# A hybrid decoder step on one core: gated outputs' parts in their own tiles, a rebuilt program end, page numbers read before the wait for old pages, key and value turns in two pairs of banks

## What is computed

```
h = RMSNorm(x);  p = h @ w_in                     # one projection for both groups
attention group (8 heads x 128): prompt: causal softmax; samples: 256 past positions from
    paged caches cache_k, cache_v (2 pages of 128 per sequence, by page_table) and the own 8
Gated DeltaNet group (8 heads x 128): causal conv + SiLU, chunked delta rule,
    gated RMSNorm with SiLU(z)
x = x + concat(attention, gated) @ w_out
x = x + ConvFFN(RMSNorm(x))                       # up, causal conv of width 3, SiLU(gate)*value, down
y = RMSNorm(x)                                    # final norm, over the 2048 channels of a token
```

## Time and profile before

| what | value |
|---|---|
| median of three runs | 1676.88 us (1676.06 to 1678.0) |
| profiled execution | 1671.89 us |
| its span, first to last instruction | 1670.2 us |
| TensorE busy | 1634.9 us (98%) |
| VectorE, ScalarE, GpSimd busy | 1048.6, 616.9, 237.4 us |
| granted TensorE clock, mean | 0.997 |
| DMA | 255.12 MB, mean 153 GB/s |

### The profile page before, as it was taken

One profiled execution on the slowest core, in us unless ns is written; L12 is line 12 of the kernel. 1 busy time (PEld: TensorE's weight loads), 2 busy tenths in 40 slices (PEclk: granted clock), 3 DMA queues, 4 the chain that ended last, 5 costly groups with the idle time before them and its releaser, 6 DMA issues.

```text
span 1670.2 us, 30879 instructions
## 1 busy us (share of the span) xinstructions
PE 1634.9 (98%) x12884; PEld 1581.8 (95%) x12884; DVE 1048.6 (63%) x1702; ACT 616.9 (37%) x783; POOL 237.4 (14%) x371
## 2 busy tenths in 40 slices
PE   8999999999999999999999999999999999999996
PEld 7999889988998888999999999999999999999996
DVE  5676688656544454676666666666666666666665
ACT  6444323432343343553333333333333333333334
POOL 1122342122211012210101010101010101010004
PEclk9999999999999999999999999999999999999998
DMA  8434355435846556454444444444444444445442
GB/s 251 126 115 116 107 152 153 116 108 171 274 137 204 176 182 190 153 157 147 151 150 152 151 152 149 148 148 151 151 151 152 147 149 148 150 149 154 141 150 83
DMA packets 230171, 255.12 MB, mean 153 GB/s; under 512 B 9036, under 2 KB 220558, under 8 KB 229712
## 3 DMA queue, kind: packets, MB, share of 16 engines
q1 hardware_dynamic: 217488, 220.16, 43.0%
q0 software_dynamic: 9856, 31.71, 6.2%
q10 hardware_dynamic: 2688, 1.27, 0.3%
HBM read 242.00 MB, written 11.12 MB: 152 GB/s over the span
## 4 chain that ended last, share of the span: by engine, by line
PE 90%; DVE 2%; issue 2%; DMA 2%; POOL 2%; ACT 0%; POOLq 0%; SPq 0%; DVEq 0%; ACTq 0%
PE ps_proj L1698 22%; PE ps_proj L1699 21%; PE ps_proj L1700 21%; PE ps_small L1699 6%; PE ps_small L1698 6%; PE ps_small L1700 6%; PE ps_small L1735 2%; DMA k_pages<-in_cache_k_dram 1%; PE ps_small L1874 0%; PE ps_small L1964 0%; PE ps_small L1864 0%; DVE state_s L1123 0%; DVE w_lo L1128 0%; DMA x_raw<-in_x_sample_dram 0%; DMA state_s<-in_state_gdn_dram 0%
## 5 line engine op out<-in xcount | busy, mean ns | idle before, releaser
L1698 PE MATMUL ps_proj<-x_hi,w_hi 128*128 128x320 f32 x2560 | 808.9, 316 | 3.4 <-issue 3.4
L1700 PE MATMUL ps_proj<-x_hi,w_lo 128*128 128x320 f32 x2560 | 791.3, 309 | 0.0
L1699 PE MATMUL ps_proj<-x_lo,w_hi 128*128 128x320 f32 x2560 | 791.2, 309 | 0.0
L791 ACT ACTIVATE w_hi<-w_raw 128x1024 fp32r<-128x1024 f32 x408 | 432.0, 1059 | 748.5 <-PE ps_proj L1700 550.6
L1128 DVE TENSOR_TENSOR w_lo<-w_raw,w_hi 128x1024 fp32r<-128x1024 f32 x408 | 498.4, 1224 | 310.5 <-ACT w_hi L791 310.1
L1698 PEld LDWEIGHTS ps_proj<-x_hi,w_hi 128*128 128x128 f32 x2560 | 481.0, 188 | 18.8 <-issue 15.6
L1699 PEld LDWEIGHTS ps_proj<-x_lo,w_hi 128*128 128x128 f32 x2560 | 481.3, 188 | 1.5 <-issue 1.4
L1700 PEld LDWEIGHTS ps_proj<-x_hi,w_lo 128*128 128x128 f32 x2560 | 480.8, 188 | 0.0
L1698 PE MATMUL ps_small<-hid_hi,w_hi 128*128 128x320 f32 x704 | 217.9, 309 | 0.0
L1700 PE MATMUL ps_small<-hid_hi,w_lo 128*128 128x320 f32 x704 | 217.6, 309 | 0.0
L1699 PE MATMUL ps_small<-hid_lo,w_hi 128*128 128x320 f32 x704 | 217.5, 309 | 0.0
(11 more groups left out here) (329 smaller groups left out, 1070.3 us busy)
## 6 DMA issues: line engine op xcount, KB each, us to landing
w_raw<-in_w_up_dram SPq DMA_DIRECT2D x176, 512.0 KB, 3.6
w_raw<-in_w_in_dram SPq DMA_DIRECT2D x112, 512.0 KB, 3.8
w_raw<-in_w_down_dram SPq DMA_DIRECT2D x88, 512.0 KB, 3.6
w_raw<-in_w_out_dram SPq DMA_DIRECT2D x32, 512.0 KB, 4.3
k_pages<-in_cache_k_dram POOLq DMA_DIRECT2D x32, 256.0 KB, 3.7
v_pages<-in_cache_v_dram POOLq DMA_DIRECT2D x32, 256.0 KB, 4.3
state_s<-in_state_gdn_dram POOLq DMA_DIRECT2D x10, 512.0 KB, 5.8
out_ss_dram<-state_s POOLq DMA_DIRECT2D x8, 512.0 KB, 4.4
```

Source lines behind the costliest of these rows:

```text
L791: act.activation(whi[:, slot], raw[:, slot], ACT.Copy).then_inc(hi_done, 1)
L1698: pe.matmul(o, hi, rhs_hi[:, k0 + kk_, :], start=first and kk_ == 0, stop=False)
L1699: pe.matmul(o, hi, rhs_lo[:, k0 + kk_, :], start=False, stop=False)
L1700: ins = pe.matmul(o, lo, rhs_hi[:, k0 + kk_, :], start=False, stop=last and kk_ == CQ - 1)
```

## The change

Four edits:

1. `mg` writes to tiles of its own. `gated_hi` lies over the keys and values of group 0's region, whose last reader is the score step of sequence 7, and `gated_lo` over `z_gate` itself. The steps stand five and three chunks before wg, and wait for that score step in place of the chunk. `fload` writes to the same place as `gated_lo`, so it moves from wg + 1 to wa0 + 1 and waits until the wg chunks are done.
2. The keys and values of units 0 and 2 are turned into banks b2 and b3, those of unit 1 into b0 and b1. The first scores wait for the copy of unit 1, and the first turn of the score weights (`T`, which writes b2) for the copy of unit 2.
3. The two page numbers are read before the wait for the old pages, and the two loads issued one behind the other.
4. The program end. `turn_y(2)` stands before the last down chunk. The last chunk signals after its first tile of 128 channels, and its two tiles are added, weighed and squared one by one. The sums over partitions are formed as columns, 128 tokens x 1, by twelve small products with the squares as the stationary operand, so no transposes follow. The root is a `Sqrt` on ScalarE, with a first `Sqrt` on constants during the last down chunks, and a reciprocal on VectorE. The rows are scaled in pieces, the last quarter straight from PSUM, and go out in six transfers in place of three.

```diff
-    slots[FIRST["wg"] - 1, PARTS - 1] += [("A", "mg", 0), ("V", "mg", 0), ("A", "mg", 1), ("V", "mg", 1)]
-    slots[FIRST["wg"] + 1, 0].append(("A", "fload"))
+    for g in range(2):
+        slots[FIRST["wg"] - 5 + 2 * g, PARTS - 1] += [("A", "mg", g), ("V", "mg", g)]
+    slots[FIRST["wa0"] + 1, 0].append(("A", "fload"))
...
+    zhi = nc.alloc_sbuf_tensor_at("gated_hi", [P, 8, TOK], F32R, offset=mixer_at + 4 * 4 * TOK)
+    zlo = nc.alloc_sbuf_tensor_at("gated_lo", [P, 8, TOK], F32R, offset=zz_at)
...
+            for ready, count, out, tile_ in (
+                    ("y0", 1, O["yp"][0, 0:P, 0:1024], yo[:, 0, 0:1024]),
+                    ("y1", 1, O["yp"][0, P:SEQ, 0:1024], yo[:, 1, 0:1024]),
+                    ("y0", 2, O["yp"][0, 0:P, 1024:2048], yo[:, 0, 1024:2048]),
+                    ("y1", 2, O["yp"][0, P:SEQ, 1024:2048], yo[:, 1, 1024:2048]),
+                    ("y0", 3, samples[:, 0:1024], yo[0:NS, 2, 0:1024]),
+                    ("y0", 4, samples[:, 1024:2048], yo[NS:P, 2, 0:1024])):
                 sp.wait_ge(fin[ready], count)
...
-                    act.activation(kst[0:n, (3 * g + t) % 2].rearrange("p h d -> p (h d)"), b0[0:n], ACT.Copy)
-                    finish(act.activation(vt[0:n, t].rearrange("p h d -> p (h d)"), b1[0:n], ACT.Copy))
+                    k_bank, v_bank = (b0, b1) if t == 1 else (b2, b3)
...
                     after(act, "V", "oz", g, 2)
-                    act.wait_ge(mm_done, FIRST["wg"])
-                    finish(act.activation(xhi[:, 8 + 4 * g:12 + 4 * g, :], zz[:, 4 * g:4 * g + 4, :], ACT.Copy))
+                    after(act, "P", "SS", 0, DB - 1)
+                    finish(act.activation(zhi[:, 4 * g:4 * g + 4, :], zz[:, 4 * g:4 * g + 4, :], ACT.Copy))
...
+            def last_tile_square(j):
+                act.wait_ge(fin["x7"], j + 1)
+                act.wait_ge(fin["sqs"], 6)
+                act.activation(sqb[:, 1, j, :], xres[:, 14 + j, :], ACT.Square).then_inc(fin["sq"], 1)
...
+            act.wait_ge(fin["ms"], 1)
+            act.activation(sm("ssx"), sm("ssx"), ACT.Sqrt).then_inc(fin["mr"], 1)
             act.wait_ge(fin["r"], 1)
-            act.wait_ge(fin["ev"], 12)
-            act.activation(yo[:, 1, :], yo[:, 1, :], ACT.Copy, scale=sm("rsx", P, 1, 2)).then_inc(fin["y1"], 1)
+            act.wait_ge(fin["ev"], 9)
+            root_ = sm("rsx", P, 1, 2)
+            act.activation(yo[:, 1, 0:1024], yo[:, 1, 0:1024], ACT.Copy, scale=root_).then_inc(fin["y1"], 1)
+            act.activation(yo[:, 1, 1024:1536], yo[:, 1, 1024:1536], ACT.Copy, scale=root_)
+            act.wait_ge(fin["t"], 11)
+            act.activation(yo[:, 1, 1536:2048], psA[:, 1, :], ACT.Copy, scale=root_).then_inc(fin["y1"], 1)
...
-                    after(pe, *(("A", "kv", g, t - 1) if t else ("V", "hb", g)))
-                    for kind, bank in ((1, b0), (2, b1)):
+                    after(pe, *(("A", "kv", g, 0) if t == 2 else ("V", "hb", g)))
+                    for kind, bank in ((1, b0 if t == 1 else b2), (2, b1 if t == 1 else b3)):
...
-                        after(pe, "A", "kv", g, 2)
+                        after(pe, "A", "kv", g, 1)
...
+                def add(x, first, last):
+                    for t, rows in ((0, slice(0, P)), (1, slice(0, P)), (2, slice(0, NS)), (2, slice(NS, P))):
+                        n, c0 = unit(t)
+                        ins = pe.matmul(token_sum(t)[rows, :], x[:, c0:c0 + n], sm("tmp", P, 0, 1), start=first, stop=last)
+                    return ins
...
+                    page = [pool.value_load(ptab[0:1, 2 * b + i:2 * b + i + 1], min_val=0, max_val=n_pool - 1) for i in range(2)]
                     if name == "pk":
...
                     for i in range(2):
-                        page = pool.value_load(ptab[0:1, 2 * b + i:2 * b + i + 1], min_val=0, max_val=n_pool - 1)
-                        src = cache[0].rearrange("n s h d -> n s (h d)")[bass.DynSlice(page, 1), :, 512 * g:512 * g + 512]
+                        src = cache[0].rearrange("n s h d -> n s (h d)")[bass.DynSlice(page[i], 1), :, 512 * g:512 * g + 512]
...
-            pool.wait_ge(fin["mr"], 1)
-            power(sm("rsx", P, 0, 2), sm("ssx", P, 0, 2), P, 2)
-            power(sm("rsx", NS, 2, 3), sm("ssx", NS, 2, 3), NS, 1).then_inc(fin["r"], 1)
```

More of the change, by code:

```diff
@@ L1098, in _ @@
                     new_rows_out(4)
+                    act.activation(sm("so", P, 0, 4), C("ones", P, 4), ACT.Sqrt)
                 elif d < 7:
@@ L1688, in finish, with products @@
                 ins.then_inc(done["P"], 1)
-            def products(c, slot, out_bank, k0, first, last, rhs_hi, rhs_lo, between=lambda r: None):
+            def products(c, slot, out_bank, k0, first, last, rhs_hi, rhs_lo, between=lambda r: None, first_tile=None):
                 pe.wait_ge(lo_done, c + 1)
@@ L1703, in products @@
                             between(done_ * PARTS // (2 * CQ) - 1)
+                    if j == 0 and first_tile is not None:
+                        ins.then_inc(first_tile, 1)
                 ins.then_inc(mm_done, 1)
@@ L2014, in step @@
                     after(pe, "V", "N", g, h)
+                    if h == 0:
+                        after(pe, "A", "kv", g, 2)
                     s_ = sc[:, h % 2]
@@ L2160, in turn_y @@
                     for j in range(4):
-                        ins = turn(psA[0:n, t, j * P:(j + 1) * P], xn[:, q % 2, j, c0:c0 + n], P)
+                        out, tile_ = psA[y_rows(t, q), t, j * P:(j + 1) * P], xn[:, q % 2, j, c0:c0 + n]
+                        if y_rows(t, q).start:
+                            ins = pe.matmul(out, tile_, C("ident"), start=True, stop=True)
+                        else:
+                            ins = turn(out, tile_, P)
                     ins.then_inc(fin["t"], 1)
             for d in range(8):
-                down(c + d, NB - 1, d, (NB - 1) % 2)
+                down(c + d, NB - 1, d, (NB - 1) % 2, fin["half"] if d == 7 else None)
                 if d == 0:
@@ L2173, in _ @@
                     turn_y(d // 2 - 1)
-            turn_y(2)
-            pe.wait_ge(fin["ne"], 5)
-            last_sum()
+                elif d == 6:
+                    turn_y(2)
+            last_sums()
             turn_y(3)
-            pe.wait_ge(fin["ms"], 1)
-            pe.wait_ge(f["add"], NB * 8 + 2)
-            for t in range(3):
-                n, c0 = unit(t)
-                ins = pe.transpose(b0[0:n, t:t + 1], rs2[0:1, c0:c0 + n], C("ident", 1, 1))
-            ins.then_inc(fin["mt"], 1)
         @block.gpsimd
```

120 lines of the change are left out of this document (80 added, 40 removed).

## The result

The changed kernel takes 1659.53 us (median of 4 runs, 1658.61 to 1660.96), the kernel before beside it 1676.47 (4 runs, 1675.29 to 1678.0). The ratio is 0.9897, 95% interval 0.9885 to 0.991. It is 16.9 us faster. The profiled execution has a span of 1659.3 us, 10.9 less than before. So profile and profile differ by about what was forecast, and the medians by more. The experiments are about that difference.

A forecast was written before the change was run, and what follows sets the result against it. TensorE was busy 1634.9 of 1670.2 us, so only its idle time and the program end could pay. Terms 3.2 + 3.0 + 0 + 2.3 + 0.2 + 2.8 = 11.5, taken as 11.4: median 1665.5 us, range 1662.5 to 1670.5.

The forecast's parts named there:

- Turns of keys and values: First scores of group 1: TensorE's wait for unit 2's copy goes whole, 3.2 us won, bounds 3.2 and 2.3.
- rival 1: Waits come back elsewhere (fload issues, score scale without cover, pages bound by bandwidth): 6.5 us won, 1670.4; chance 0.17.
- Gated parts: Start of wg: TensorE's 2.99 us idle, caused by VectorE's subtractions, goes; 3.0 us won, bounds 3.0 and 0.
- rival 4: At wg the 2.99 us idle are issue and stay: 8.4 us won, 1668.5; chance 0.04.
- Moved loads: fload's ten issues on ScalarE, ahead of the key copy: value 0, 0.7 us of cover; bounds 0 and 2 us lost.
- Page numbers: TensorE's four waits for key pages shrink through earlier reads and loads: 2.3 us won, bounds 3.3 and 1.0.
- Program end: Behind TensorE's last product: scaling and first transfer start sooner, 0.2 us added for shorter rows; 2.8 us won, bounds 4.0 and 1.0.
- rivals 2 and 3: Rival 2: program end gives nothing, 1668.2 us, chance 0.07. Rival 3: output pieces do not overlap, 1687.5 us, chance 0.02.
- I subtract the same microseconds from both: Whole kernel: the same savings, 11.4 us, taken from the profiled execution (1671.89 us) and from the runs' median (1676.88).
- value pages: TensorE's wait for value pages, 0.2 us, likely gone too, since the first is issued 0.9 us sooner.

The follow-up runs named there:

- the three sets: Runs of the unchanged kernel before, timed beside three groups of four follow-up kernels each: medians 1675.84, 1676.31 and 1675.68 us.
- Gated parts and banks: Kernel before with only the first and second edits, key pages and program end as before: 1665.63 us, ratio 0.9941.
- the parts alone: Kernel before with one edit each: gated parts 1673.05 us, key and value banks 1671.22, page numbers 1673.44, program end 1672.86.

## Why the prediction was right or wrong

**Right: the waits and the end.** Turns of keys and values: 3.2 forecast, the wait is gone; rival 1's lack of cover for the score scale did not come. Gated parts: 3.0 forecast, 3.0 gone (the other 0.4 us of that row stays, ahead of wa1), and the cause was VectorE, so rival 4 falls. Moved loads: 0 forecast, 0.7 us of cover forecast and 0.7 found. Page numbers: 2.3 forecast, 3.3 less 1.0 is 2.3. That it fits so well is luck: these waits sum to 2.2 to 3.3 us in the profiles with the old order and to anything from 0 to 2.1 in those with the new one. Program end: 2.8 forecast, 3.1 found; scaling 3.1 behind the last product forecast, 3.0 found; first issue to end 9.0 forecast, 8.95 found (to the end of the span, where the forecast counted to the last landing). The 0.2 us added for shorter rows stands in no row, and the drain grew no longer. So rivals 2 and 3 fall.

The Trainium skill (DMA: Bandwidth & Descriptors, "Anatomy of one DMA — SWDGE (gpsimd) path") gives each transfer a fixed part of about 2.0 us, from which I had estimated 6 us lost for six transfers taken one after another. The page says it of transfers that GpSimd issues, one by one; these are issued by SyncE, together. Here the fixed parts lie on top of each other: 8.95 us for six against 9.14 for three, each to the end of the span, for the same 2.62 MB.

**Near by profile, in part by luck.** The span fell by 10.9 against 11.4 forecast, but the changed kernel's execution had lost 1.75 us at its start. From the first projection on it is 12.7 us shorter. The repeated changed kernel has a span of 1656.7 and takes the first projection out at 47.68, so 14.0 less from there on; it has no wait for key pages at all.

**Wrong: the step "I subtract the same microseconds from both", and with it the price of a gap.** I noted that the median of before lay 5.0 us above the profiled execution, and treated that as a constant. It was not one. And the two long gaps stand in the sum at their idle time, 3.0 and 3.2 us, with nothing for what follows them, because in the one execution that I read nothing did. Together they are worth 9.9 us in place of 6.2. The runs of the kernel before in the three sets, by their mean clock:

| mean clock | 0.993 | 0.994 | 0.995 | 0.996 | 0.997 |
|---|---|---|---|---|---|
| runs | 13 | 21 | 17 | 9 | 5 |
| mean us | 1678.3 | 1676.7 | 1675.5 | 1674.4 | 1674.2 |

A line through all 67 (these and one each at 0.992 and 0.998) gives 1.1 us for each 0.001. One stretch of 3.4 us at 0.50 takes half its length, 1.7 of 1670 us, so 0.001, from the mean. That the line has 1.1, where the rows above have 1.4 to 1.5 a stretch, can come of stretches that lie partly over idle time and of the program end; no run separates these. For the mean clock also counts the end, where TensorE has nothing left to do and a low clock costs nothing. The first profile, at 0.997, had no low stretch ahead of its end:

```profile
1660.00:1670.00 10.00, 0.00 (x0) 0.00 (x0) 2.21 (x2) 1.74 (x1) 0.00 (x0) 0.53 0.74 262
```

That is 9.5 us at 0.50 to the end of the span, and the other profiles with the old end have 8.2 to 9.8. So 0.9946, the mean of the 67, is between two and three stretches more than the end's. "Gated parts and banks" has the old end too: its 0.9974 is 0.0028 above the kernel before, 3.1 us by the line. With 6.2 us of waits and twice the 0.27 that is 9.8, where 9.9 were measured.

The changed kernel's nine runs have 0.9974 as well, but its own two profiles have only 3.9 and 5.3 us at 0.50 at their end, and 0.0013 or more of its higher clock can be that. For the whole change I therefore take the two changed profiles without low stretches, 12.7 and 14.0 us shorter than the first profile from the first projection on, and an estimate of 1.5 to 3 us for the clock (the line's 1.1 for the 0.0015 that are left, or two stretches at 1.5). That makes 14 to 17, where 15.1 and 16.9 were measured. In 12.7 are the terms (3.2, 3.0, 2.3, 3.1 and some 0.2 of value pages, 11.8) and the 0.27 for each gap gone.

Of the 3.7 to 5.5 us that the forecast missed, the low clock is then about half, and these runs don't give its share more sharply. The range was too narrow for the same reason: its lower end left 3 us for anything that I had not seen, and the 5.0 us between profile and median, a number in my own text, was the sign that something of that size varied from run to run. Of those 5.0 us, a little over 1 lies at the start: the first projection is taken out at 47.14 there, and at 47.31 to 49.49 in the thirteen other profiles, in most of them between 47.7 and 48.9.

The Trainium skill (TensorE: Matmul & The Clock Gate, "HAM oscillation — how this bites in real kernels") takes the extra time of a throttled stretch as half of its length. Here the trace agrees within what the copies' spacing can tell: 1.5 us for 3.4 us, and 1.4 in the kernel before. I had not weighed that page, since the profile of before showed a clock of 1.00 around both gaps.

**What stays open.** Not every long gap is followed by a low stretch: in the profiles with a gap of 2.99 us or more behind the program's start, two such gaps in the first profile of before had none, the twelve others did. Between 1.1 and 3.0 us no gap was put in on purpose; behind the one of 1.72 us in the earlier trace rows the clock stayed at 1.00. Low stretches at 112 to 118 and at 269 to 287, in the delta rule's small products, come and go with no gap ahead of them. No kernel here was made to remove those. And the parts alone add up to some 12 us, the whole wins 15 to 17, while taken out of the whole three of them cost 4.4, 5.4 and 3.9 us. Whether a part is worth more within the whole is not shown: the intervals cover the difference, and the mean clocks of the kernels with one gap back (0.9966 and 0.9962) lie close to that of the changed kernel beside them (0.9970).

## What to carry to other kernels

Where TensorE is otherwise full, price an idle gap of about 3 us at its length, plus 0.27 us that the view doesn't count, plus 1.5 us for the clock behind it (2.6 was seen); six gaps of 1.1 us cost only the first two. Before subtracting terms of a profile from a median, ask why the two differ: the mean clock of every run is in the results, and here 0.003 of it went with 3 us. But take off first what the clock does where TensorE has no work left. And before comparing the spans of two profiles, line them up at a row behind the program's start: here that moved the difference from 10.9 to 12.7 us.

## What the runs showed of the hardware that was not expected

A gap of 3.4 us in a block of nothing but 320-column products was followed by 3.4 us at 1.2 GHz. The fall comes up to 1.3 us after work has resumed (732.4 against 731.11) or while the engine still idles (759.7 against 760.79), so some of it costs nothing. Reading both page numbers first makes two issues of 0.56 us each with no time between them, where a read between them took 0.60.
